# A two-block layer on one core: folded Fourier transform, earlier state-space steps, attention weights scaled by VectorE

## The reference

```python
h = rms_norm(x, g_pre_mix) * (1 + sc_m) + sh_m
u, f, q, k, v = jnp.split(h @ w_in, splits, axis=-1)     # widths 384, 256, 384, 128, 128
y = concatenate([s5_mixer(u, ...), fourier_mixer(f, w_fft), window_attention(q, k, v, sink)]) @ w_out

def s5_mixer(u, ...):       # 24 groups of 16 channels, 64 complex states, both directions
    ...                     # h[t] = lam_bar * h[t-1] + b_bar u[t]; y = Re(c h) + d_skip * u
    y = gelu(y)
    return y * sigmoid(y @ w_glu)

def fourier_mixer(f, w_fft):        # 4 heads of 64
    mixed = jnp.fft.fft2(ff, axes=(1, 3), norm='ortho').real
    return einsum('bshd,hde->bshe', mixed, w_fft)

def window_attention(q, k, v, sink):    # 6 query heads on 2 key heads, blocks of 128, band of 384 keys
    scores = where(valid, q k^T * 64**-0.5 + bias, -1e30)
    m = maximum(max(scores), sink)
    p = exp(scores - m)
    p = p / (sum(p) + exp(sink - m))
    return p @ v
```

## Time and profile before

| | |
|---|---|
| median of 3 runs | 2736.72 us (2732.39 to 2737.16) |
| profiled execution | 2729.13 us, span 2727.3 us, granted clock 0.986 |
| TensorE busy | 2613.6 us |
| VectorE busy | 1460.0 us |
| ScalarE busy | 1028.4 us |
| GpSimd busy | 1095.9 us |

### The profile page before, as it was taken

One profiled execution on the slowest core, in us unless ns is written; L12 is line 12 of the kernel. 1 busy time (PEld: TensorE's weight loads), 2 busy tenths in 40 slices (PEclk: granted clock), 3 DMA queues, 4 the chain that ended last, 5 costly groups with the idle time before them and its releaser, 6 DMA issues.

```text
span 2727.3 us, 31627 instructions
## 1 busy us (share of the span) xinstructions
PE 2613.6 (96%) x12542; PEld 2082.2 (76%) x12542; DVE 1460.0 (54%) x1881; ACT 1028.4 (38%) x1600; POOL 1095.9 (40%) x605
## 2 busy tenths in 40 slices
PE   6789989999999999999999999999999999999997
PEld 3657757777888878877777788888788888888885
DVE  5646657697778722265756432433556655422225
ACT  4412654464544411345454331211354433312112
POOL 1322114346666554452211133322353655534444
PEclk8999999999999999999999999999999999999998
DMA  6444257322222333232123122111424232423322
GB/s 249 179 140 109 74 179 285 116 70 69 83 89 82 119 127 148 86 132 73 47 70 116 55 80 77 49 49 49 141 92 154 85 116 101 155 103 145 112 81 85
DMA packets 109619, 297.92 MB, mean 109 GB/s; under 512 B 13344, under 2 KB 28192, under 8 KB 109472
## 3 DMA queue, kind: packets, MB, share of 16 engines
q1 hardware_dynamic: 102592, 275.36, 29.6%
q10 hardware_dynamic: 3456, 10.73, 1.0%
q0 software_dynamic: 3424, 9.81, 1.0%
HBM read 233.09 MB, written 62.76 MB: 108 GB/s over the span
## 4 chain that ended last, share of the span: by engine, by line
PE 70%; DVE 5%; POOL 2%; ACT 1%; issue 1%; DMA 1%; SPq 0%; POOLq 0%; DVEq 0%; ACTq 0%
PE ps L1698 15%; PE ps L1700 15%; PE ps L1699 15%; PE ps L1732 5%; PE ps L1734 5%; PE ps L1733 5%; PE pc L1732 1%; PE pc L1734 1%; PE pc L1733 1%; PE pss L2026 1%; POOL whl L3448 1%; PE pc L2078 1%; PE pc L2080 1%; PE pc L2079 1%; DVE pad L2104 0%
## 5 line engine op out<-in xcount | busy, mean ns | idle before, releaser
L3448 POOL TENSOR_TENSOR whl<-wraw,whl 128x1024 fp32r<-128x1024 f32 (+2 forms) x309 | 648.4, 2104 | 1217.8 <-ACT whl L2918 1217.4
L1698 PE MATMUL ps<-act,whl 128*128 128x512 f32 x1824 | 732.3, 401 | 35.1 <-DVE act L2098 8.3
L1699 PE MATMUL ps<-act,whl 128*128 128x512 f32 x1824 | 714.5, 392 | 0.0
L1700 PE MATMUL ps<-act,whl 128*128 128x512 f32 x1824 | 714.3, 392 | 0.0
L1698 PEld LDWEIGHTS ps<-act,whl 128*128 128x128 f32 x1824 | 344.8, 189 | 132.1 <-issue 38.5
L2918 ACT ACTIVATE whl<-wraw 128x1024 fp32r<-128x1024 f32 (+2 forms) x309 | 267.8, 868 | 443.5 <-PE ps L1700 359.0
L1700 PEld LDWEIGHTS ps<-act,whl 128*128 128x128 f32 x1824 | 344.9, 189 | 73.4
L1699 PEld LDWEIGHTS ps<-act,whl 128*128 128x128 f32 x1824 | 345.4, 189 | 72.5 <-issue 4.1
L2098 DVE TENSOR_TENSOR y<-y,ps 128x512 f32<-128x512 f32 x176 | 121.0, 688 | 359.1 <-PE ps L1700 358.9
L1698 PE MATMUL ps<-hid,whl 128*128 128x512 f32 x544 | 214.4, 394 | 0.4
L1700 PE MATMUL ps<-hid,whl 128*128 128x512 f32 x544 | 212.2, 390 | 0.0
(11 more groups left out here) (402 smaller groups left out, 4205.9 us busy)
## 6 DMA issues: line engine op xcount, KB each, us to landing
wraw<-in_w_in SPq DMA_DIRECT2D x63, 512.0 KB, 3.3
wraw<-in_f1u SPq DMA_DIRECT2D x72, 256.0 KB, 2.8
wraw<-in_f2d SPq DMA_DIRECT2D x36, 512.0 KB, 3.3
wraw<-in_w_out SPq DMA_DIRECT2D x32, 512.0 KB, 3.3
x<-in_w_ada SPq DMA_DIRECT2D x32, 512.0 KB, 7.2
hid<-hscr SPq DMA_DIRECT2D x29, 512.0 KB, 6.5
xs<-y SPq DMA_DIRECT2D x24, 512.0 KB, 6.3
wraw<-in_f2u SPq DMA_DIRECT2D x48, 256.0 KB, 3.1
```

The source lines that it names most:

```text
L1698: pe.matmul(PSB[g.bank][:, :], hi, x_hi, start=e == 0, stop=False)
L1699: pe.matmul(PSB[g.bank][:, :], hi, x_lo, start=False, stop=False)
L1700: m = pe.matmul(PSB[g.bank][:, :], lo, x_hi, start=False, stop=e == len(ks) - 1)
L3448: return g_.tensor_tensor(out, a, b, op)
```

## The change

The order of panels becomes 8, 9, 0, 1, 2, 6, 7, 3, 4, 5. `split 3` is issued between the two halves of the head. `tab_k` and `tab_ko` are parted by a yield, and the tables' steps are planned 2.0 apart, not 2.6. The Fourier transform is folded: VectorE's new `fft_eo` forms the even and odd parts of f over positions, `fft_c` and `fft_s` run over four pieces with four dft tiles, loaded all at once after panel 8; position 512 is taken separately (`fft_n`) and added in `fft_out`. Fourier stands after panel 2. The 16 loads of U are issued before the tables end (`u_load`), the state-space steps are planned closer, and `Cb` has two buffers. In the attention `att_diag` is gone; `att_norm` multiplies the probabilities by the reciprocal, and `att_t` is a plain transposition.

```diff
-W_IN_ORDER = (0, 1, 2, 8, 9, 6, 7, 3, 4, 5)
+W_IN_ORDER = (8, 9, 0, 1, 2, 6, 7, 3, 4, 5)
...
                         self.put("ev", t)
-                        if half:
+                        if half and i == first[-1]:
+                            late = (n, t)
+                        elif half:
                             self.panel_done(n, t)
                         yield (i, t) if half else None
+                    while half == 0 and self.splits < NW:
+                        self.split()
...
-        def made_k(b0):
+        def turn_k(b0):
             p.put("tab_k", b0)
             p.put("tab_wst", b0)
+
+        def made_k(b0):
             p.put("tab_ko", b0)
             p.put("tab_kst", b0)
 
@@ -479,14 +489,20 @@
             p.put("tab_v", b0)
             p.put("tab_vst", b0)
             if n:
-                made_k(b0 - GB)
+                turn_k(b0 - GB)
             yield
             p.put("tab_w", b0)
+            if n > 5:
+                made_k(b0 - GB)
             yield
             if n < 6:
                 p.put("tab_cs", n)
                 p.put("tab_cst", n)
+                if n:
+                    made_k(b0 - GB)
                 yield
+        turn_k(NG - GB)
...
     def ssm():
+        while ("tab_cst", 5) not in p.had or n_us[0] < 3:
+            yield 1.0
+        p.put("u_load")
         while not made():
             yield 1.0
         p.put("ssm_load")
-        yield 14.0
+        yield 7.0
         p.pe(1.8, "ssm_x", 0)
         p.put("ssm_r", 0)
         yield 1.0
         for b in range(6):
             p.put("ssm_rot", b, 0)
-            yield 1.5
+            yield 1.2
             p.put("ssm_rot", b, 1)
-            yield 2.5
+            yield 1.8
...
-                p.put("att_diag", u - 2)
+                pass
...
     def fourier():
-        p.put("fft_w", p.hold[0])
-        for tp in range(8):
-            p.pe(0.9, "fft_c", tp, p.hold[1])
+        for tp in range(4):
+            p.pe(0.9, "fft_c", tp, p.hold[0], p.hold[1])
             p.poll()
-        for tp in range(8):
+        p.pe(0.5, "fft_n")
+        for tp in range(4):
             p.pe(3.4, "fft_s", tp, p.hold[2], p.hold[3])
             p.poll()
-        p.pe(3.4, "fft_mid")
+        p.pe(1.8, "fft_mid")
...
     def tables_left():
         for _ in tab:
-            yield 2.6
+            yield 2.0
...
+                if r[0] == 1:
+                    p.pe(1.8, "fft_w")
+                elif r[0] == 2:
+                    fourier()
+            if r[0] == 8:
+                p.put("fft_load")
+            if r[0] in (8, 9):
+                p.put("fft_eo", r[0] - 8)
...
-                    w.wait_ge(*done("attA", "diag", u, g))
+                    w.wait_ge(*done("attD", "scale", u, g))
                     if u:
                         w.wait_ge(*done("attA", "pt", u - 1, g))
                     elif g == 0:
                         w.wait_ge(*done("attA", "v", 0))
                     for s in range((hi - lo) // 128):
-                        m = pe.matmul(PSB[tb][:, s * 128:s * 128 + 128], scb[u % 3][:, g, s * 128:s * 128 + 128],
-                                      dgs[u % 2][:, g, :], start=True, stop=True)
+                        m = pe.transpose(PSB[tb][:, s * 128:s * 128 + 128], scb[u % 3][:, g, s * 128:s * 128 + 128], ident[:, :])
...
+            def fft_c(tp, *hold):
                 w.wait_ge(*done("fftD", "wc"))
-                if tp == 1:
-                    w.wait_ge(*done(*hold))
-                if tp >= 2:
+                if tp < 2:
+                    w.wait_ge(*done(*hold[tp]))
+                else:
                     w.wait_ge(*(done("fftA", tp - 2) if tp % 2 else done("fftD", "c", tp - 2)))
+                c = slice(tp * 128, tp * 128 + 128)
                 for pr in range(2):
-                    w.wait_ge(*z_done(8 + pr))
-                    m = pe.matmul(PSB[tp % 2][:, pr * 256:pr * 256 + 256], fT[:, pr, tp * 128:tp * 128 + 128],
-                                  WC[:, pr, :, :].rearrange("p a b -> p (a b)"), start=True, stop=True)
+                    w.wait_ge(*done("fftD", "eo", pr))
+                    for i, part in enumerate((fe, fT)):
+                        q = pr * 256 + i * 128
+                        m = pe.matmul(PSB[tp % 2][:, q:q + 128], part[:, pr, c], WC[:, pr, i, :], start=True, stop=True)
                 m.then_inc(*mark("fft", "c", tp))
 
+            def fft_n():
+                for pr in range(2):
+                    m = pe.matmul(PSS[:, 0, 2 + pr:3 + pr], WC[:, pr, 0, :], fT[:, pr, 512:513], start=True, stop=True)
+                m.then_inc(*mark("fft", "n"))
...
-                                      dft[tp % 4][:, i * 512:i * 512 + 512], start=tp == 0, stop=tp == 7)
+                                      dft[tp][:, i * 512:i * 512 + 512], start=tp == 0, stop=tp == 3)
...
+                w.wait_ge(*done("attD", "recip", u))
+                lo, hi = span(UNITS[u][1])
+                for g in range(2):
+                    sc = scb[u % 3][:, g, 0:hi - lo]
+                    v.tensor_scalar(sc, sc, sm[:, 10 + g:11 + g], None, ALU.mult).then_inc(*mark("attD", "scale", u, g))
...
+            def fft_eo(pr):
+                f, back, e = fT[:, pr, 1:512], fT[:, pr, 1023:512:-1], fe[:, pr, :]
+                w.wait_ge(*z_done(8 + pr))
+                v.tensor_copy(e[:, 0:1], fT[:, pr, 0:1]).then_inc(*step("fftD"))
+                tt(e[:, 1:512], f, back, ALU.add).then_inc(*step("fftD"))
+                w.wait_ge(*last("fftD"))
+                tt(f, f, back, ALU.subtract).then_inc(*mark("fftD", "eo", pr))
...
+                ts(st[:, 0:512:2], Pb[:, 0:512:2], n512, ALU.add).then_inc(*step("fftD"))
+                ts(st[:, 1:512:2], Pb[:, 1:512:2], n512, ALU.subtract).then_inc(*mark("fftD", "a", pr))
...
-            def att_diag(u):
-                w.wait_ge(*done("attD", "recip", u))
-                if u >= 2:
-                    w.wait_ge(*done("att", "t", u - 2, 1))
-                for g in range(2):
-                    av(dgs[u % 2][:, g, :], ident[:, :], ACT.Copy, scale=small[:, u % 3, 10 + g:11 + g]).then_inc(
-                        *mark("attA", "diag", u, g))
...
-                    if b:
-                        w.wait_ge(*done("ssmD", "h2", b - 1))
-                    q.dma_start(Cb[:, :, :, :], t["cscr"][:, :, b * NB:b * NB + NB, :]).then_inc(*dmark("d_lc", b))
+                    if b > 1:
+                        w.wait_ge(*done("ssmD", "h2", b - 2))
+                    q.dma_start(Cbs[b % 2], t["cscr"][:, :, b * NB:b * NB + NB, :]).then_inc(*dmark(f"d_lc{b % 2}", b))
...
+            def u_load():
                 for n in (4, 5):
                     w.wait_ge(*done(f"d_cs{n % 2}", n))
                 for i in range(3):
                     w.wait_ge(*done(f"d_us{i}"))
-                load_w(0)
-                load_c(0)
                 for part, (g0, n) in enumerate(((0, 8), (8, NG - 8))):
```

More of the change, by code:

```diff
@@ L341, in gemm @@
         first = idxs[:head]
+        late = None
         if first and not pre:
@@ L488, in tables @@
                 p.put("tab_cst", n)
+                if n:
+                    made_k(b0 - GB)
                 yield
+        turn_k(NG - GB)
+        yield
         made_k(NG - GB)
@@ L549, in ssm @@
             p.put("ssm_scan", b, 0)
-            yield 2.0
+            yield 1.4
             if b < 5:
@@ L651, in modulation @@
         p.had.add("x_again")
-    p.beside(tables_left(), 22.0)
+    p.beside(tables_left(), 18.0)
     p.beside(ssm())
@@ L2084, in tensor @@
                      "tab_ko": tab_ko, "ssm_x": ssm_x, "ssm_y": ssm_y, "glu": glu, "att_v": att_v, "att_score": att_score,
-                     "att_t": att_t, "att_out": att_out, "fft_w": fft_w, "fft_c": fft_c, "fft_s": fft_s, "fft_mid": fft_mid,
+                     "att_t": att_t, "att_out": att_out, "fft_w": fft_w, "fft_c": fft_c, "fft_n": fft_n, "fft_s": fft_s, "fft_mid": fft_mid,
                      "r_rows": r_rows, "r_bc": r_bc, "r_rows2": r_rows2, "r_bc2": r_bc2, "lru_ri": lru_ri, "pool": pool, "hg_v": hg_v,
@@ L2895, in vector @@
                      "ssm_rot": ssm_rot, "ssm_scan": ssm_scan, "ssm_back": ssm_back, "glu_out": glu_out,
-                     "att_score": att_score, "att_norm": att_norm, "att_split": att_split, "fft_w": fft_w, "fft_c": fft_c,
+                     "att_score": att_score, "att_norm": att_norm, "att_split": att_split, "fft_eo": fft_eo, "fft_w": fft_w, "fft_n": fft_n, "fft_c": fft_c,
                      "fft_out": fft_out, "fft_split": fft_split, "nsum": nsum, "r_fac": r_fac, "r_add": r_add, "r_sum": r_sum, "r_fac2": r_fac2,
@@ L3167, in att_split, with fft_c @@
                 av(A[:, 0, 5 + i, HALF[half]], qT[:, i, HALF[half]], ACT.Copy).then_inc(*mark("attA", "hi", i, half))
-            def fft_c(tp, hold):
+            def fft_c(tp, *hold):
                 if tp % 2:
@@ L3741, in fft_load @@
                 for tp in range(4):
-                    load_d(tp)
```

(7 more changed lines are left out.)

106 lines of the change are left out of this document (52 added, 54 removed).

## The result

The changed kernel takes 2688.69 us (median of 4 runs, 2688.28 to 2690.95) against 2736.94 us (4 runs, 2732.39 to 2738.58): a ratio of 0.9832, 95% interval 0.9816 to 0.9848. The forecast was 2697, with 2677 to 2716 as its range. The span of the profiled execution fell from 2727.3 to 2686.5 us, 40.8 us. What these 7.5 us are no trace shows.

The account below looks back on a forecast made before the run. TensorE, busy 96% of the span, was taken as the bound; -24 (tables, Fourier), -9 (state space, attention) and -7 (gate) made -40, from 2729.13 to 2689, plus 7.6 for the median: 2696.7 us, range 2677 to 2716.

Parts of the forecast that it names:

- Stage 1: Tables and Fourier, 79.5 to 198.0 us: next w_in matmul starts at 174.2, not 198.0, so -24.
- The charge for splits: Tables and Fourier: POOL's six splits each delay VectorE's table chain by 2.08 us, 12.5 in all.
- the last tab_w then ends at 154.1: End of VectorE's table chain, summed from its steps, folds, copies and splits; TensorE's remaining work was added behind it.
- Stage 2: State space and attention, 198.0 to 369.8 us: 17.4 us less TensorE work, partly lost to idle growth, -9.
- The transposes: Attention: 132 plain transposes at 0.14 us replace diagonal matmuls at 0.27, TensorE does 17.4 us less.
- They cost TensorE nothing directly: State space: VectorE's five waits for Cb, 18.5 us, go, without direct gain for TensorE.
- What I described: Attention: transposes wait for scales behind VectorE's state-space operations, TensorE's idle time growing from 7.3 to 16 us.
- Rival C: VectorE becomes the bound in state space and attention: +4 there (0 to +8), total -27, 2710 us; chance 0.22.
- Stage 3: Gate of the state-space branch, 369.8 to 413.66 us: hi copy starts some 7 us earlier, -7.
- B: Tables and Fourier: splits don't stall VectorE, so 36 us gained there, total 2677 us; chance 0.20.
- D: Attention: transposes still cost 0.27 us like diagonal matmuls, total -26, 2711 us; chance 0.05.
- E: Attention: transposes wait for scales behind state-space operations, 2.2 us a unit, 53 back, 2750 us; chance 0.04.

Follow-up runs that it names:

- e6: Changed kernel with POOL's subtraction of splits 4 to 8 cut to 8 of 1024 columns, leaving out low parts of five weight panels: 2681.13 us.
- e10: Changed kernel with each matmul of fft_s issued twice, VectorE's fold kept: 2705.36 us.
- e8: Changed kernel with fft_w's copy and two copies of fft_c on ScalarE in place of VectorE: 2692.0 us.
- e1: Changed kernel with the attention as before: ScalarE makes scaled diagonals, TensorE multiplies with them, VectorE does not scale: 2702.1 us.
- e4: Changed kernel with one Cb buffer again, each batch's load of factors behind the batch before: 2713.11 us.
- e2: Kernel before the change with only the attention's part added (plain transposes, scale by VectorE): 2733.9 us, ratio 0.9985 to 1.0005.
- e5: Changed kernel with the old, wider spacing of the state-space steps: 2704.13 us.

## Why the prediction was right, and where its terms were off

**Stage 1, -24, measured -19.0.** The mechanism held in kind: VectorE's chain holds TensorE up (e6), and Fourier's TensorE work behind it counts in full (e10). The charge for splits was right: six stretches with 2.18, 2.12, 2.07, 2.40, 2.6 and 0.95 us over, 12.3, against 12.5 in the sum. Mis-sized was "the last tab_w then ends at 154.1": it ended at 160.5. The sum had the chain without waits; VectorE waited 7.4 us in it (3.5 for tab_ko to release the tables, 1.8 and 1.4 for fft_c and fft_w, 0.8 for panel 9's copy). Started 0.6 us earlier, 78.9 + 57 + 3.0 + 0.7 + 1.4 + 12.3 + 7.4 is 160.7. The part behind it was 18.5, not 20.1.

That the sum runs over the last tab_w was itself a wrong step. TensorE did not wait for it: tab_k 21 follows with no idle time ahead:

```profile
161.84 0.82 PE L1810 MATMUL pc<-ident,tab 128*128 128x128 f32 x6
```

The last step that waited for the chain was tab_k 15, at 143.83; from there TensorE had work without a break of more than 0.4 us until 175.8, and then the wait of 3.25 for fT. What shortens the chain ahead of that step shows in the stage: tab_k 15 came 6.4 us earlier in e6 and 2.0 in e8, and the stage ended 6.9 and 1.7 earlier. The waits at tab_k were 8.46 at 9 (forecast 9), 4.89 at 15 (forecast 3), none at 18 (forecast 2.5), and 3.34 at 3, which the forecast did not have.

Told from TensorE's side, -19.0 is 17.4 us less work and 1.6 less idle time. Fourier's three groups gave 21.0 (41.5 to 20.5), as forecast; but the other 560 or so instructions of the stage took 58.4 us, not 54.8, at a granted clock of 0.90, not 0.93. The sum had no term for that.

The Trainium skill ("SBUF — State Buffer", "SBUF: two separate sides") calls the port pair an exclusive lock held for a whole instruction: the trace agrees, with delays of 2.07 to 2.6 us (once 0.95) beside subtractions of 2.5 to 2.8, and rows of 0.56 where e6 has none.

**Stage 2, -9, measured -13.7.** Two terms were off and partly cancel. The transposes gave 15.2 us, not 17.4 (0.156 each in their stretch, not 0.14). And TensorE's idle time did not double: in the stretch of the units (228.8 to 331.1, the counterpart of the earlier trace rows) it was 7.0 us, before 7.3, where the sum let it grow to 16. "They cost TensorE nothing directly", said of the waits for Cb, fits the kernel before (e1 has neither the waits nor the scale on VectorE, and 171.2) but not the changed one: there one buffer costs 21 us (e4). What I described did happen in e2, where the scale meets the old state space, with 19.2 us idle. What keeps it away is two buffers (e4) and narrower spacing (e5, 7.6 us). VectorE does much of its state-space work from 190 to 215, busy for 24.0 of 25 us (window of all engines):

```profile
190.00:215.00 25.00, 25.00 (x169) 20.92 (x169) 24.00 (x32) 4.29 (x6) 8.80 (x5) 1.00 0.36 105
```

Three of the six batches are scanned before the first score at 229, in e2 and e5 two; and the last scan starts 41 us ahead of the attention's end (before 13, in e5 16), so the last units have VectorE for themselves. So the part that looked like the gain, the transposes, needs the part that looked like housekeeping; in stage 2 neither gives more than 0.6 us without the other. Rival C is refuted as a bound of the changed kernel (e1, and only 2.7 us of TensorE's waits there are for VectorE's scores and scales), but is the right description of e2.

**Stage 3, -7, measured -5.6.** The cause is the early end of the state space, as said (e5 gives the old 44.8 back). The detail differed: the modulation's rows still stand ahead of the product, from 348.43, but they end before it is due. It is TensorE, in order behind w_out's first matmuls, that sets the first sigmoid (354.31), and the hi copy stands in ScalarE's queue behind the second one (357.38; 20.3 us after the attention's end, said 18).

**Rivals B, D and E.** Splits do stall VectorE (B falls). Plain transposes cost little over half (D falls). TensorE waited 1.0 us in all for sc in the changed kernel (E falls); its slack was there because the state space was not.

**The sum.** -19.0 - 13.7 - 5.6 = -38.3, and 2.5 of chance, beside the forecast -40. That the total was this close owes something to errors of opposite sign, 5 too much in stage 1 and 5 too little in stage 2. The median is 8 us below the forecast of 2697, mostly because that added the 7.6 us by which the profiled execution of the kernel before lay below its own median.
